# Prompt attention: reciprocals of the softmax sums spread over the partitions by a store and two broadcast loads, in place of a copy, a product with the unit matrix and an eviction

## The reference, cut to what matters

```python
logits = einsum('bthd,btkhd->bthk', q, k_sel) * HEAD_DIM ** -0.5
logits = logits + bias
logits = where(valid, logits, -inf)
p = softmax(logits, axis=-1)
return einsum('bthk,btkhd->bthd', p, v_sel)
```

## Time and profile before

| what | value |
|---|---|
| median of the runs shown | 2200.75 us (2200.16 to 2202.24) |
| the profiled execution's own time | 2201.84 us |
| its span | 2200.2 us |
| mean granted clock of TensorE | 0.973 |
| prompt attention in it | 586.8 to 732.4 us, 145.6 us |
| busy in that stretch | PE 130.1, weight loads 90.5, DVE 99.3, ACT 90.6, POOL 59.5 us |
| busy in the whole span | PE 2056.8 us (93%), DVE 1265.9 (58%), ACT 711.6 (32%), POOL 547.4 (25%) |

### The profile page before, as it was taken

The page is one execution under the profiler, slowest core; times in us unless marked ns, Lnnn a source line. Parts: engine busy times, 40 slices in busy tenths (PEclk is TensorE's granted clock), DMA queues, the critical chain, the costliest instruction groups (busy, mean ns, idle before and its releaser), DMA issues.

```text
span 2200.2 us, 33028 instructions
## 1 busy us (share of the span) xinstructions
PE 2056.8 (93%) x12955; PEld 1905.2 (87%) x12955; DVE 1265.9 (58%) x2056; ACT 711.6 (32%) x1045; POOL 547.4 (25%) x428
## 2 busy tenths in 40 slices
PE   5999999999889879798899999999999999999997
PEld 5969889889756549776799999999999999999997
DVE  5789899899276634335344455344544445444555
ACT  4343333323366421134232223222232222322233
POOL 0323334112243231210122222222222222222220
PEclk9999999999899789899899999999999999999998
DMA  5202222323210253332111111111111111111123
GB/s 149 63 29 87 78 86 80 95 85 96 74 65 2 88 147 120 115 125 77 39 49 49 47 51 39 49 45 43 49 49 46 42 48 49 44 44 49 49 87 113
DMA packets 176802, 150.59 MB, mean 68 GB/s; under 512 B 29594, under 2 KB 150842, under 8 KB 176514
## 3 DMA queue, kind: packets, MB, share of 16 engines
q1 hardware_dynamic: 175370, 144.20, 21.4%
q0 software_dynamic: 1280, 4.20, 0.6%
HBM read 119.50 MB, written 27.95 MB: 67 GB/s over the span
## 4 chain that ended last, share of the span: by engine, by line
PE 44%; DVE 4%; issue 2%; DMA 0%; DVEq 0%; SPq 0%
PE ps L58 44%; DVE f_acc L2493 1%; DVE g_fT L2525 1%; DVE f_acc L2502 1%; DVE f_acc L2494 1%; DMA f_x<-d_x 0%; PE ps L2637 0%; DVE f_x L2578 0%; PE ps L2629 0%; DVE f_acc L2533 0%; DVE g_fT L2523 0%; DVE f_acc L2509 0%; DVEq L2520 0%; DVEq L2493 0%; PE ps L2620 0%
## 5 line engine op out<-in xcount | busy, mean ns | idle before, releaser
L58 PE MATMUL ps<-g_xT_h,f_wh 128*128 128x344 f32 x1536 | 492.9, 321 | 7.2 <-issue 5.0
L58 PE MATMUL ps<-g_xT_l,f_wh 128*128 128x344 f32 x1536 | 491.4, 320 | 0.0
L58 PE MATMUL ps<-g_xT_h,f_wl 128*128 128x344 f32 x1536 | 491.2, 320 | 0.0
L2367 POOL TENSOR_TENSOR f_wl<-f_wst,f_wh 128x1024 fp32r<-128x1024 f32 x94 | 245.9, 2616 | 383.1 <-ACT f_wh L2413 383.1
L58 PEld LDWEIGHTS ps<-g_xT_h,f_wh 128*128 128x128 f32 x1536 | 289.1, 188 | 9.1 <-issue 7.3
L58 PEld LDWEIGHTS ps<-g_xT_h,f_wl 128*128 128x128 f32 x1536 | 289.3, 188 | 0.0
L58 PEld LDWEIGHTS ps<-g_xT_l,f_wh 128*128 128x128 f32 x1536 | 289.2, 188 | 0.0
L1092 PE MATMUL ps<-g_hT_h,j_wh 128*128 128x344 f32 (+1 forms) x840 | 285.4, 340 | 0.0
L1092 PE MATMUL ps<-g_hT_l,j_wh 128*128 128x344 f32 (+1 forms) x840 | 268.7, 320 | 0.0
L1092 PE MATMUL ps<-g_hT_h,j_wl 128*128 128x344 f32 (+1 forms) x840 | 268.7, 320 | 0.0
L58 PE MATMUL ps<-f_gh,f_wh 128*128 128x344 f32 x768 | 248.9, 324 | 7.5 <-DVE g_fT L2525 6.9
(11 more groups left out here) (428 smaller groups left out, 3355.2 us busy)
## 6 DMA issues: line engine op xcount, KB each, us to landing
f_wst<-in_w_up SPq DMA_DIRECT2D x64, 512.0 KB, 4.0
j_wst<-in_w_in SPq DMA_DIRECT2D x34, 512.0 KB, 4.6
f_wst<-in_w_down SPq DMA_DIRECT2D x32, 512.0 KB, 3.6
d_gates<-j_ring SPq DMA_DIRECT2D x16, 516.0 KB, 3.0
m_gt<-d_gates SPq DMA_DIRECT2D x16, 516.0 KB, 4.8
a_k<-in_cache_k SPq DMA_DIRECT2D x16, 256.0 KB, 2.8
o_wst<-in_w_o SPq DMA_DIRECT2D x8, 512.0 KB, 3.8
o_x<-in_x_prompt SPq DMA_DIRECT2D x8, 512.0 KB, 4.8
```

What stands on the lines that cost most here:

```text
L58: mm = pe.matmul(ps[0:m, 3 * slot + c, 0:CH], w[:, k, 0:m], x[:, k, c * CH:(c + 1) * CH], start=(first and k == 0 and n == 0), stop=(last ...
L2367: pool.tensor_tensor(wl[:, s, :], wst[:, s, :], wh[:, s, :].bitcast(F32), ALU.subtract).then_inc(w_lo, 1)
```

## The change

The ring keeps only the halves of the exponentials. `rq`, the copy on POOL, the product on PE and the copy on ACT go. SP stores the two columns of `rden` to a scratch tensor in HBM (`d_rden`, 128 partitions with two numbers each, written as two rows of 128, so every number on its own) and, when that has landed, reads each row back to 64 partitions of `rb` (four buffers in place of two). y_norm waits for these two transfers. The page loads and the loads for the next phase go into the same loop of SP, one for each pair, between the store and the broadcasts; `tab_in` is awaited in pair 0, behind the first store.

```diff
-        rq = sb("rq", [P, 2, 2, HD])
-        rb = sb("rb", [P, 2, P])
+        RB = 4
+        rb = sb("rb", [P, RB, P])
...
+        rd_out = [sem(f"rd_out{i}") for i in range(2)]
+        rb_in = [sem(f"rb_in{i}") for i in range(RB)]
...
-        SPREAD = 2
-        halves = [k for n in range(NPAIR)
-                  for k in [(n, e, f) for f in range(1 + (n // 4 >= 4)) for e in range(2)] + [(n, 0, SPREAD)]]
+        halves = [(n, e, f) for n in range(NPAIR) for f in range(1 + (n // 4 >= 4)) for e in range(2)]
...
-            sp.wait_ge(tab_in, 16)
-            for b in range(NS):
-                for q in range(2):
...
+            def store_reciprocals(n):
+                sp.wait_ge(r_done, 2 * n + 2)
+                sp.dma_start(g.d_rden[n].rearrange("e q -> q e"), rden[:, 2 * n:2 * n + 2],
+                             allow_slow_non_contiguous=True).then_inc(rd_out[n % 2], 16)
+
+            def spread_reciprocals(n):
+                sp.wait_ge(rd_out[n % 2], 16 * (n // 2 + 1))
+                if n >= RB:
+                    sp.wait_ge(yn_done, n - RB + 1)
+                for e in range(2):
+                    sp.dma_start(rb[e * HD:(e + 1) * HD, n % RB, :], g.d_rden[n, e, :].partition_broadcast(HD)).then_inc(rb_in[n % RB], 16)
...
+            for n in range(NPAIR):
+                store_reciprocals(n)
+                if n == 0:
+                    sp.wait_ge(tab_in, 16)
+                if n < 2 * NS:
+                    index_page(*divmod(n, 2))
+                elif n - 2 * NS < len(later):
+                    sp.dma_start(*later[n - 2 * NS]).then_inc(next_in, 16)
+                spread_reciprocals(n)
...
-                pool.wait_ge(r_done, 2 * n + 2)
-                if n >= 2:
-                    pool.wait_ge(turned, turn_no[n - 2, 0, SPREAD] + 1)
-                pool.tensor_copy(rq[:, n % 2, :, :], over(rden[:, 2 * n:2 * n + 2], HD)).then_inc(rq_done, 1)
...
-            def r_copy(n):
-                act.wait_ge(turned, turn_no[n, 0, SPREAD] + 1)
-                if n >= 2:
-                    act.wait_ge(yn_done, n - 1)
-                act.activation(rb[:, n % 2, :], r_cols(n), ACT.Copy).then_inc(pt_done[0], 1)
...
-                dve.wait_ge(pt_done[0], copies(n, 0, SPREAD))
-                dve.tensor_tensor(yn[:, n % 2, :], y_cols(n), rb[:, n % 2, :], ALU.mult).then_inc(yn_done, 1)
+                dve.wait_ge(rb_in[n % RB], 32 * (n // RB + 1))
+                dve.tensor_tensor(yn[:, n % 2, :], y_cols(n), rb[:, n % RB, :], ALU.mult).then_inc(yn_done, 1)
...
-            def spread(n):
-                pe.wait_ge(rq_done, n + 1)
-                ring_free(turn_no[n, 0, SPREAD])
-                pe.matmul(r_cols(n), rq[:, n % 2, :, :].rearrange("p e d -> p (e d)"), g.ident[:, :],
-                          start=True, stop=True).then_inc(turned, 1)
```

More of the change, by code:

```diff
@@ L1340, in phase_attention @@
         v0_in, v_in, m_ready, mb_done = (sem(n) for n in ("v0_in", "v_in", "m_ready", "mb_done"))
-        s_done, l_done, nmx_done, e_done, r_done, rq_done, turned, y_done, yn_done, yh_done, yl_done = (
-            sem(n) for n in ("s_done", "l_done", "nmx_done", "e_done", "r_done", "rq_done", "turned", "y_done",
+        s_done, l_done, nmx_done, e_done, r_done, turned, y_done, yn_done, yh_done, yl_done = (
+            sem(n) for n in ("s_done", "l_done", "nmx_done", "e_done", "r_done", "turned", "y_done",
                              "yn_done", "yh_done", "yl_done"))
         pt_done = [sem(f"pt_done{e}") for e in range(2)]
+        rd_out = [sem(f"rd_out{i}") for i in range(2)]
+        rb_in = [sem(f"rb_in{i}") for i in range(RB)]
         tab_in, kx_in, next_in, kept = (sem(n) for n in ("tab_in", "kx_in", "next_in", "kept"))
@@ L1360, in y_cols @@
             return ps[:, YB, 0:P]
-        def r_cols(n):
-            return ps[:, bank(turn_no[n, 0, SPREAD]), 0:P]
         def copies(n, e, f):
@@ L1385, in _ @@
             sp.dma_start(g.table[:, :], g.page_table.rearrange("b n -> (b n)").unsqueeze(0)).then_inc(tab_in, 16)
-            sp.wait_ge(tab_in, 16)
-            for b in range(NS):
-                for q in range(2):
-                    page = sp.value_load(g.table[0:1, 2 * b + q:2 * b + q + 1], min_val=0, max_val=g.cache_k.shape[0] - 1)
-                    sp.dma_start(g.kx[:, b, q, :], g.cache_kidx[bass.ds(page, 1), :, :].rearrange(
-                        "a p c -> p (a c)")).then_inc(kx_in, 16)
@@ L1393, in _, with index_page @@
[L1393 to L1398, removed]
+            def index_page(b, q):
+                page = sp.value_load(g.table[0:1, 2 * b + q:2 * b + q + 1], min_val=0, max_val=g.cache_k.shape[0] - 1)
+                sp.dma_start(g.kx[:, b, q, :], g.cache_kidx[bass.ds(page, 1), :, :].rearrange(
+                    "a p c -> p (a c)")).then_inc(kx_in, 16)
@@ new lines, in _ @@
+            later = [(g.own[:, :], g.c_own), (g.ownT32[:, :], g.c_own32), (g.ownT64[0:NS * H, :], g.c_own64),
+                     (g.ownT64[NS * H:P, :], g.c_own64), (g.hsel[0:NS * H, :], g.c_headsel), (g.hsel[NS * H:P, :], g.c_headsel),
+                     (g.jsel[ID:ID + JH, :], g.c_jsel), (g.rel_s[:, :], g.rel_bias), (g.onehot_s[:, :], g.c_onehot_s),
+                     (g.gT[:, :, :], g.d_g), (g.w_glu_st[:, :, :], g.w_glu.rearrange("(k p) n -> p k n", p=P))]
+            for n in range(NPAIR):
[7 more added lines that the diff above has]
+                spread_reciprocals(n)
@@ L1465, in _ @@
                     pt_copy(n - 1, 1, 1)
-                if 1 <= n < NPAIR + 1:
-                    r_copy(n - 1)
                 if 3 <= n < NPAIR + 3:
@@ L1594, in _ @@
                     turn(n - 1)
-                    spread(n - 1)
 def phase_late(nc, g):
@@ L2721, in build @@
     g.d_qs = scratch("d_qs", (NS, AW))
+    g.d_rden = scratch("d_rden", (NT * H // 2, 2, P))
     g.d_x2 = scratch("d_x2", (T, D))
```

## The result

The changed kernel takes **2376.2 us** (median of 4 runs, 2373.11 to 2378.67) beside 2200.72 for the kernel before: 1.0795 times as long, with a 95% interval of 1.0780 to 1.0809. The forecast was 2205.5 us, range 2198.5 to 2222. The direction was forecast, the size was not: +175.5 us in place of +4.8, far outside the range.

The account below looks back on a forecast made before the run. Prompt attention was read alone, between barriers: a loop through y_norm and weigh up to tile 3, PE from tile 4 on. Start and SP's period, +11.8 us, less 7.0 gained, gave +4.8: 2205.5 us, range 2198.5 to 2222.

Parts of the forecast that it names:

- the size of the store's landing: SP's store of 256 single numbers to HBM in each pair: issue to landing taken as 2.3 us.
- the forecast's own sum: SP's period for each pair: store landing 2.3, two broadcast issues 1.2, semaphores and gaps 0.2, together 3.7 us.
- The two rows that bounded it: Profile rows for the landing: 8 KB in rows of 256 bytes, 1.5 us; a load of 1024 single numbers, 4.7.
- The upper end: Store landing at 4.7 us: SP's period 6.1, total over 2250 us; left out of the range.
- The mechanism: Prompt attention: SP handles pairs one after the other, y_norm waits for the broadcasts; start and period together +11.8 us.
- a period set by SP beyond pair 15: Sign that would show the forecast wrong; SP's period was expected to bind up to about pair 10.
- The rival of the slow store: Single numbers land in 3.1 us, SP's period 4.5 binds through tile 4: 2217.6 us; chance 0.22.
- The start: First store lands behind V's load, so y_norm(0) comes at 600.35 in place of 593.43: +6.9 us.
- The gain: Spreading product leaves PE's path from tile 4 on: 13 pairs by 0.40, 3 by 0.66 us; -7.0 us.
- The covers at the end: Stage's end: gT's load, the last pair's store and broadcasts, and b_l stay hidden behind other work; nothing added.
- The clock: Rival: TensorE's clock stays low as PE idles then works in gaps, costing 6.4 us: 2211.9; chance 0.10.
- the sum of the stage: Prompt attention: start and period +11.8 us, product removed from PE -7.0, together +4.8 us.

Follow-up runs that it names:

- x2: Changed kernel storing only head 0's reciprocals of each pair, 128 numbers in place of 256, which both broadcasts read; 2366.51 us.
- x8: Changed kernel storing 128 rows of 512 bytes (unit matrix) in place of the single numbers, broadcasts reading rows of x_prompt; 2210.92 us (1.0048).
- x1: Changed kernel with neither product nor transfers: rb set to 1 once, division by the sums left out; 2202.31 us (1.0010).

## Why the prediction was wrong

**The step that failed is the size of the store's landing**: "a quarter of these numbers, so I take 1.5 + (4.7 - 1.5)/4 = 2.3". It is 8.3 us, and the forecast's own sum with it, 8.3 + 1.2 + 0.2 = 9.7 us, is the measured period. The two rows that bounded it lacked what decides: the rows of 256 bytes aren't single numbers, and the 1024 single numbers of the same rows are a load, whose target is on the chip. The upper end was not one, and the end that was named, 4.7 us and over 2250, was put out of the range by the count of the numbers. x2 shows that the count is not what it goes by. The landing made the period 9.6 us in place of 3.7, and 32 pairs at that pace fill 308 of the 315.5 us of a stage that took 145.5.

**The mechanism was right.** SP's period sets the pace, DVE is idle before y_norm until the broadcasts land, and PE behind it; the sign to look for, "a period set by SP beyond pair 15", is there to the end. The rival of the slow store was this one with 3.1 us for it. The rule cited beside it, from the Trainium skill's page "DMA: Bandwidth & Descriptors", section "Rules for kernel authors", that a strided last dimension becomes one descriptor for each element, is borne out by packets of 4 bytes, 9 ns each; but they are sent in about a microsecond, so the count is not what cost.

The 2.0 us of fixed cost that the prediction takes from the Trainium skill's page "DMA: Bandwidth & Descriptors", section "Anatomy of one DMA", stand there for transfers that GpSimd issues; this store is SP's, and 2.0 would have missed 8.3 us as well.

**The start**, +6.9, measured +6.8 in x8, in part by luck: the broadcasts went out at 597.07, 0.8 us sooner than forecast, and took 2.5 us in place of 1.8. In the changed kernel y_norm(0) came at 605.30: V landed at 600.35 and the store, issued at 590.48 behind it, only at 602.15.

**The gain**, -7.0, measured -5.7. From pair 16 to pair 28 the forecast's 0.40 and 0.66 us make 5.6, and x1 gained 5.3; from pair 28 to 31 it gained only 0.3. The products of pairs 30 and 31 have no scores behind them, which the forecast counted nearly in full. Before tile 4 nothing was forecast; y_norm(0) to y_norm(16) takes 57.6 us in x1 and 57.2 before, which agrees. ACT's and POOL's copies were costed at nothing, and x1, which drops them, shows nothing more to gain.

**The covers at the end** held, as the earlier trace rows answered above shows, with room from the longer stage. In x8, which has no such room, pairs 16 to 31 take the same 74.8 us as in x1.

**The clock** stays low, as a consequence. Stretches of the kernel after, against the earlier trace rows (columns as there):

```profile
602.00:605.00 3.00, 0.00 (x0) 0.00 (x0) 0.00 (x0) 0.00 (x0) 0.00 (x0) 0.50 0.13 22
650.00:700.00 50.00, 21.85 (x102) 13.09 (x104) 13.48 (x57) 10.05 (x30) 7.91 (x12) 0.57 0.23 12
...
750.00:800.00 50.00, 31.72 (x234) 24.07 (x232) 19.88 (x62) 17.59 (x46) 11.10 (x16) 0.77 0.11 8
```

PE, busy for under half of the time, was granted 0.50, the lower of its two levels (1.2 GHz), at the start and 0.57 on average, so mostly that level, from 650 to 700 us, where it had 1.00 (2.4 GHz) before. Beside SP's period this can have cost little: DVE's idle time ends with the broadcasts in 27 of 32 pairs all the same. In x8 the clock was still 0.53 from 610 to 620 us and 1.00 from 620; the 2.1 us lost from pair 0 to pair 16 contain it.

**What was not in the forecast at all** is the feed-forward part's 7 us. The text let every microsecond outside the stage pass, because the phases are behind barriers. With x8's store the sum of the stage, +4.8, would have been right to 1.5 us, partly by luck, since the forecast has 2.8 us too much for the period and 1.3 too much for the gain; and the time would still have been 5 us too low.

## What to carry to other kernels

A transfer's price is its landing, and that must come from a row of the same kind: same target, same piece size, same neighbours; where there is none, the open end belongs into the range, and a chain that waits for it once per pair multiplies it. Don't write single 4-byte numbers side by side into HBM and wait for them: gather them on the chip first, or keep them 64 bytes apart. And when instructions are taken from TensorE's program ahead of a loop, compare the loop's "issue" stops before crediting or blaming the edit.

## What the runs showed that was not expected

- A store of 256 single numbers to 1 KB of HBM lands after 8.3 us, about 6 of them after its last packet, with no read of that HBM needed for it (the first store shows it); at 64 or 512 bytes apart the same numbers land after 2.0 us, in on-chip memory side by side after 3.0.
- A page load behind such a store lands after 7.2 us in place of 1.8; in the pair shown its last packet is through by 712.5, 2.5 us before it lands.
- 96 idle instructions on TensorE, ahead of a loop that they have nothing to do with, made the program 7 us longer (1.0029, 1.0013 to 1.0045), by one more stop of about 1.1 us in each round; 48 did nothing. Differences of 0.3% between two kernels can be of this kind.
